# Expert rows moved by DMA through DRAM instead of by one-hot products, in a two-block transformer kernel

## Chip, cores and metric

One core of a Trainium2 chip runs the kernel. The metric is the device time in microseconds of one execution; three runs of the kernel before gave 2006.03, 2007.79 and 2010.1 us, so the median is 2007.79 us.

## What is computed

The reference runs 256 tokens of width 1024 through two transformer layers of one model and one layer of a second, all in float32. The part that the change touches is the feed-forward of the second layer, a mixture of experts: each token goes to two of eight experts, the tokens of an expert are collected in blocks of 128 rows, each block is multiplied by its expert's weights, and the results are weighted and added back to their tokens.

```python
logits = (xt @ w_router).astype(jnp.float32)
top_logit, top_idx = lax.top_k(logits, TOP_K)
gates = jax.nn.softmax(top_logit, axis=-1)
...
dest = pad_start[sorted_e] + (jnp.arange(A, dtype=jnp.int32) - start[sorted_e])
tok_buf = jnp.full((rows,), T, jnp.int32).at[dest].set((order // TOP_K).astype(jnp.int32))
gate_buf = jnp.zeros((rows,), jnp.float32).at[dest].set(gates.reshape(-1)[order])
...
xs = xt_pad[tok_buf].reshape(n_blocks, EXPERT_BLOCK, D)

def expert_block(args):
    xb, e = args
    return swiglu(xb, w_gate[e], w_up[e], w_down[e])

ys = lax.map(expert_block, (xs, block_expert)).reshape(rows, D)
ys = ys * gate_buf[:, None].astype(ys.dtype)
out = jnp.zeros((T + 1, D), ys.dtype).at[tok_buf].add(ys)[:T]
```

The expert width is 3584, so an expert has 42 units of weights of 1 MB. The inputs shown here need eight blocks, one for each expert; up to eleven are provided for.

## The kernel before, in words

**Precision.** Every large product is made from three products of a shorter type: SyncE loads a unit of weights (128x2048) into one of six slots of `raw`, ScalarE writes its high part `wh` (L922 in the expert loop, L638 elsewhere), VectorE subtracts to get the low part `wl` (`rest`, L1495), and TensorE multiplies high by high, low by high and high by low (L1047 to L1049). The high and low parts have three slots. SyncE may refill a slot when the split of its unit is done (`lo_ready`); ScalarE may split unit j+3 when TensorE is done with unit j (`unit_done`); TensorE waits for `lo_ready` of each unit.

**Order of work.** All engines have their instructions written out in order. Attention and feed-forward (L1223 to L1228, called FFN0 here) of the first layer come first; between FFN0's units SyncE also loads 24 units `ada` for VectorE's modulation vectors (L1691), which use the same ring. FFN0's list of loads runs g0 u0 g1 u1 d0 ada0 ada1 ada2 g2 u2 d1 ada3 ada4 g3 u3 d2. Then come the second layer's convolution and attention, its router, and the expert loop, followed by the second model.

**Before the loop.** `z_tok` (tokens in rows) comes from transposes (`ztok`). VectorE works out for each token's two assignments a row number `kcol`, 128 times the block plus the row in it. TensorE turns `kcol` and the gates `gcol` into rows (`as_rows`, L1300, for `krow` and `grow`).

**One-hot products.** `select` (L1842 to L1854) compares `kcol` with 0 to 127, giving a matrix `sel` with a one where a token belongs to a row of this block, then takes 128 off `kcol` for the next block. `gather` (L1306 to L1311) multiplies `z_tok` by `sel`, 16 products of 128x128 in two halves (banks `G0`, `G1`), and leaves the block's rows transposed in PSUM; ScalarE and VectorE split them into `xgh` and `xgl`. For the way back, VectorE builds `scat` (L1925 to L1932), a matrix of gates at the places of the tokens, and `scatter` (L1324 to L1328) multiplies the block's result `y_tok` by it: eight products of 128x256 in four groups (`S0` to `S3`). VectorE adds each group to the residual `hT` (L1907).

**The loop** (TensorE L1332 to L1401, ScalarE L916 to L945, VectorE L1889 to L1938, SyncE L531 to L535) runs over the blocks. A block has seven chunks c; each has two units of gate (g), two of up (u) and, one chunk later, two of down (d) weights: g0 u0 g1 u1 d0 g2 u2 d1 and so on to d6, each in two halves. After the first gate units of the next chunk TensorE transposes the hidden state (`turned`, L1354, banks `T0` to `T6`), ScalarE takes its high and VectorE its low part. The scatter groups of the block before stand behind the up units of chunks 0 to 3 (L1391 to L1395); both gather halves for the next block stand behind `d5` (L1396 to L1401), the second of them in the PSUM bank that the last transpose `T6` used, so that it waits until VectorE has drained it. At the end of a block ScalarE copies the result from PSUM into `y_tok` (L944). After the loop TensorE scatters the last block (L1403 to L1409), and POOL, ScalarE and VectorE go on with the second model.

POOL does nothing in the loop: it clears `y_tok` and `scat` at L599 and L600, and its next instruction (L603) waits for the last scatter.

## Time and profile before

| | before |
|---|---|
| runs | 2006.03, 2007.79, 2010.1 us |
| median | 2007.79 us |
| span of the profiled execution | 2008.4 us |
| TensorE busy | 1882.3 us, 94% |
| VectorE busy | 1484.6 us, 74% |
| ScalarE busy | 1173.2 us, 58% |
| POOL busy | 177.5 us, 9% |
| DMA of SyncE's queue | 497.24 MB, 65.7% of 16 engines' span |
| chain that ended last | TensorE 83%, VectorE 7%, ScalarE 5% |
| mean granted TensorE clock | 0.971 of full |

For the profiled execution no time of its own is given beside its span; the span is 0.6 us above the median of the runs. Busy times count overlapping matmuls once. "Idle before" is the time an engine stood still ahead of an instruction, with the instruction whose end released it. A float32 matmul shows as two records, one of the shorter type or a transpose as one. Times of instructions are microseconds from the start of the span.

### The profile page before, as it was taken

Reading aid. Unit: us, or ns where it says so; the run is one execution under the profiler, and the core shown is the slowest. Engines: PE = TensorE matmul, PEld = TensorE weight load, DVE = VectorE, ACT = ScalarE, POOL = GpSimd, SP = SyncE. Lnnn points to the kernel's source line nnn. Section 1 sums busy time; section 2 is a strip of 40 time slices with the busy share of each in tenths; the row PEclk is TensorE's granted clock in tenths of the full one; section 3 lists DMA queues with packets and bytes.
Section 4 is the critical chain, followed back from the end, with each engine's and each line's share of the span. In section 5 each row is a group of like instructions: output and inputs, shape, how many; then the busy total and the mean of one; then the engine's idle time right before and its main releaser. Section 6 shows DMA issues by size and latency. Waiting matters only on the chain.

```text
span 2008.4 us, 28246 instructions
## 1 busy us (share of the span) xinstructions
PE 1882.3 (94%) x10934; PEld 1656.0 (82%) x10934; DVE 1484.6 (74%) x1406; ACT 1173.2 (58%) x1143; POOL 177.5 (9%) x156
## 2 busy tenths in 40 slices
PE   6988999999789999999999999999999979679997
PEld 6977999998778788788787887878878879569997
DVE  6856777667668979798797897887979845665554
ACT  5445434448446767767676777767777744643332
POOL 3032111211000000000000000000000000312221
PEclk8999999999879999999999999999999979999999
DMA  7404788730239979899798998997989934024540
GB/s 296 135 14 158 280 328 335 273 126 1 105 126 354 368 297 355 313 357 364 305 347 327 351 361 310 359 371 293 357 310 361 367 130 167 23 105 161 178 166 22
DMA packets 69052, 499.89 MB, mean 249 GB/s; under 512 B 7664, under 2 KB 7792, under 8 KB 8432
## 3 DMA queue, kind: packets, MB, share of 16 engines
q1 hardware_dynamic: 68688, 497.24, 65.7%
q0 software_dynamic: 288, 1.57, 0.2%
q8 instruction: 55, 0.90, 0.2%
q14 instruction: 21, 0.17, 0.0%
HBM read 497.73 MB, written 1.05 MB: 248 GB/s over the span
## 4 chain that ended last, share of the span: by engine, by line
PE 83%; DVE 7%; ACT 5%; issue 3%; POOL 1%; DMA 0%; DVEq 0%; ACTq 0%; SPq 0%
PE ps L1047 24%; PE ps L1049 24%; PE ps L1048 24%; ACT wh L922 2%; DVE wl L1495 2%; PE ps L1327 2%; PE ps L1249 2%; PE ps L1070 2%; PE ps L1309 1%; DVE big L1488 1%; PE ps L1354 1%; POOL xl L556 1%; PE ps L1178 1%; DVE al L1495 1%; PE ps L1199 1%
## 5 line engine op out<-in xcount | busy, mean ns | idle before, releaser
L1495 DVE TENSOR_TENSOR wl<-raw,wh 128x2048 fp32r<-128x2048 f32 x446 | 1021.4, 2292 | 321.2 <-ACT wh L638 177.2
L922 ACT ACTIVATE wh<-raw 128x2048 fp32r<-128x2048 f32 x336 | 643.0, 1918 | 229.8 <-PE ps L1049 229.8
L1047 PE MATMUL ps<-wh,xh 128*128 128x512 f32 (+1 forms) x1040 | 398.1, 383 | 2.6 <-DVE wl L1495 2.6
L1049 PE MATMUL ps<-wh,xl 128*128 128x512 f32 (+1 forms) x1040 | 390.7, 376 | 0.0
L1048 PE MATMUL ps<-wl,xh 128*128 128x512 f32 (+1 forms) x1040 | 389.7, 375 | 0.0
L1047 PE MATMUL ps<-xh,wh 128*128 128x256 f32 x1184 | 346.1, 292 | 30.4 <-POOL xl L556 14.5
L1048 PE MATMUL ps<-xl,wh 128*128 128x256 f32 x1184 | 341.4, 288 | 0.0
L1049 PE MATMUL ps<-xh,wl 128*128 128x256 f32 x1184 | 341.2, 288 | 0.0
L638 ACT ACTIVATE wh<-raw 128x2048 fp32r<-128x2048 f32 x107 | 204.2, 1910 | 175.0 <-PE ps L1049 171.1
L1047 PEld LDWEIGHTS ps<-xh,wh 128*128 128x128 f32 x1184 | 233.0, 197 | 35.8 <-issue 30.0
L1048 PEld LDWEIGHTS ps<-xl,wh 128*128 128x128 f32 x1184 | 233.1, 197 | 1.7 <-issue 1.7
L1049 PEld LDWEIGHTS ps<-xh,wl 128*128 128x128 f32 x1184 | 232.6, 196 | 0.0
L1047 PEld LDWEIGHTS ps<-wh,xh 128*128 128x128 f32 x1040 | 195.9, 188 | 41.2 <-DVE wl L1495 7.2
L1049 PEld LDWEIGHTS ps<-wh,xl 128*128 128x128 f32 x1040 | 195.8, 188 | 36.1
L1048 PEld LDWEIGHTS ps<-wl,xh 128*128 128x128 f32 x1040 | 196.0, 189 | 34.4 <-issue 1.0
L1047 PE MATMUL ps<-wh,ah 128*128 128x512 f32 x448 | 181.7, 406 | 1.6 <-DVE al L1495 1.6
L1049 PE MATMUL ps<-wh,al 128*128 128x512 f32 x448 | 175.4, 391 | 0.0
L1048 PE MATMUL ps<-wl,ah 128*128 128x512 f32 x448 | 175.0, 391 | 0.0
L1047 PE MATMUL ps<-ah,wh 128*128 128x256 f32 x432 | 122.4, 283 | 0.2 <-POOL al L587 0.2
L1048 PE MATMUL ps<-al,wh 128*128 128x256 f32 x432 | 122.3, 283 | 0.0
L1049 PE MATMUL ps<-ah,wl 128*128 128x256 f32 x432 | 122.3, 283 | 0.0
L550 POOL MEMSET big<- 128x4096 f32 (+1 forms) x3 | 8.0, 2665 | 1082.4 <-DVE hT L1670 1082.1
(276 smaller groups left out, 2161.1 us busy)
## 6 DMA issues: line engine op xcount, KB each, us to landing
raw<-in_experts SPq DMA_DIRECT2D x336, 1024.0 KB, 4.8
raw<-in_units SPq DMA_DIRECT2D x134, 1024.0 KB, 5.1
big<-in_mem SPq DMA_DIRECT2D x1, 1024.0 KB, 7.1
hT<-in_x SPq DMA_DIRECT2D x1, 1024.0 KB, 9.1
big<-in_mem POOLq DMA_DIRECT2D x1, 1024.0 KB, 7.1
out<-sqz SPq DMA_DIRECT2D x2, 512.0 KB, 2.6
cst<-in_constants SPq DMA_DIRECT2D x1, 752.5 KB, 14.4
big<-in_c POOLq DMA_DIRECT2D x1, 512.0 KB, 7.9
```

The source lines that it names most:

```text
L556: pool.tensor_tensor(xl[:, k, :], src[:, k, :], xh[:, k, :].bitcast(F32), ALU.subtract).then_inc(sem("norm_lo_pool"), 1)
L638: act.activation(wh[:, p % SPL, :], raw[:, n % RAW, :], ACT.Copy).then_inc(sem("hi_ready"), 1)
L922: act.activation(wh[:, p % SPL, :], raw[:, n % RAW, :], ACT.Copy).then_inc(sem("hi_ready"), 1)
L1047: mm(out_, lh, rh, start=start, stop=False, **kw)
L1048: mm(out_, lh, rl, start=False, stop=False, **kw)
L1049: return mm(out_, ll, rh, start=False, stop=stop, **kw)
L1070: ins = mm(bank(f"nsum{k}")[:, 0:T], ones, src[:, T * j:T * j + T], start=(j == 0), stop=(j == KT - 1))
L1178: ins = mm(s[:, at:at + nk], m["q"][:, P * t:P * t + P], m["k"][:, 0:nk], start=True, stop=not fox)
L1199: mm(o[:, 0:T], m["v"][0], pT[:, 0:T], start=not second, stop=False, skip_group_check=True)
L1249: mm(bank(f"conv{c}")[:, 0:T], diag[:, n % DIAG_RING, :], upad[:, c, tap:tap + T], start=(tap == 0), stop=(tap == TAPS - 1)).then_inc(sem( ...
L1327: ins = mm(psum[:, T * c:T * c + T], y_tok[:, P * o:P * o + P], scat, start=True, stop=True)
L1495: return V.tensor_tensor(out_, whole, leading.bitcast(F32), ALU.subtract)
```

## The change

Rows go through two new tensors in DRAM, `x_rows` and `y_rows`, of twelve blocks of 128 rows each. Only the first block is still gathered with a one-hot product, and only the last is still scattered with one.

- SyncE fills all twelve blocks of `x_rows` and five of `y_rows` with zeros, in two DMAs from a cleared stretch of SBUF, behind the load of `u2` in FFN0. POOL's clearing of the convolution's padding now covers 1716 columns in place of 180.
- Before the loop POOL scatters the token rows to `x_rows` in four indirect DMAs (two assignments by two halves of the tokens).
- In each block SyncE stores the result of the block before (behind its thirteenth load) and loads the rows of the next block into `x_blk` (behind its twenty-first). TensorE turns these with eight transposes where the gather stood. The scatter groups, the token adds and the per-block `select` and `scat` work are gone from the loop; `scat` is made once before it, for the last block.
- During the last block POOL gathers every assignment's result row from `y_rows` (four indirect DMAs), scales by the gates, with zero for rows of the last block, and adds both; TensorE adds these tokens transposed into the banks of the last scatter.
- `as_rows("krow")` now stands behind the first gather; `select` no longer waits for it. The last scatter's groups use the banks 6, 7, 4, 5.

The core of the diff:

```diff
@@ SyncE
                 load(n)
+                if n == NUMBER["u2"]:
+                    sp.wait_ge(sem("upad_zeroed"), 1)
+                    sp.dma_start(x_rows.rearrange("a p f -> p a f"),
+                                 zeros.unsqueeze(1).broadcast_to([P, MAXBLK + 1, D])).then_inc(sem("rows_zeroed"), 16)
+                    sp.dma_start(y_rows[E - 1:MAXBLK + 1, :, :].rearrange("a p f -> p a f"),
+                                 zeros.unsqueeze(1).broadcast_to([P, MAXBLK + 2 - E, D])).then_inc(sem("rows_zeroed"), 16)
...
                 load_expert(j, slice(0, 1))
+                if j == 20:
+                    sp.wait_ge(sem("x_scattered"), 16 * 2 * TT)
+                    sp.dma_start(x_blk, x_rows[1:2, :, :].rearrange("a p f -> p (a f)"))
...
                     load_expert(j, bass.ds(e, 1))
+                    if j == 12:
+                        sp.wait_ge(sem("moe_y"), i * 2 + 3)
+                        sp.dma_start(y_rows[bass.ds(i, 1), :, :].rearrange("a p f -> p (a f)"), y_tok)
+                    if j == 20:
+                        sp.wait_ge(sem(f"moe_filled{b}"), i * per + use + 1)
+                        sp.dma_start(x_blk, x_rows[bass.ds(i + 2, 1), :, :].rearrange("a p f -> p (a f)"))
@@ POOL
-            pool.memset(y_tok, 0.0).then_inc(sem("moe_y"), 1)
-            pool.memset(scat, 0.0).then_inc(sem("moe_scat"), 1)
+            pool.wait_ge(sem("rows_zeroed"), 32)
+            pool.wait_ge(sem("moe_rows"), 1)
+            for a in range(2):
+                for t in range(TT):
+                    pool.indirect_dma_start(x_by_row, IndirectOffsetOnAxis(kidx[:, a, t:t + 1], 0), z_tok[:, t, :], None)
...
+            pool.wait_ge(sem("y_stored"), last * 16 + 1)
...
+            for t in range(TT):
+                for a in range(2):
+                    pool.indirect_dma_start(y_got[a][:, t, :], None, y_by_row, IndirectOffsetOnAxis(yidx[:, a, t:t + 1], 0))
+            for t in range(TT):
+                pool.wait_ge(sem(f"y_got{t}"), 32)
+                pool.tensor_scalar(y_got[0][:, t, :], y_got[0][:, t, :], gkept[:, 0, t:t + 1], None, ALU.mult)
+                pool.tensor_scalar(y_got[1][:, t, :], y_got[1][:, t, :], gkept[:, 1, t:t + 1], None, ALU.mult)
+                pool.wait_ge(sem("y_gated"), 2 * t + 2)
+                pool.tensor_tensor(y_kept[:, t, :], y_got[0][:, t, :], y_got[1][:, t, :], ALU.add)
@@ ScalarE
+                act.wait_ge(sem("y_stored"), i * 16 + 1)
                 for g in range(2):
                     act.activation(y_tok[:, 512 * g:512 * g + 512], ps[:, 4 + g, :], ACT.Copy)
@@ TensorE
+            def tokens_of_earlier_blocks(psum, j):
+                for c in range(2):
+                    o = 2 * j + c
+                    for t in range(TT):
+                        at = T * c + P * t
+                        mm(psum[:, at:at + P], y_kept[:, t, P * o:P * o + P], ident, start=(c == 0 and t == 0), stop=False,
+                           skip_group_check=True)
...
+                def next_rows(g):
+                    psum, done = spare(f"G{g}")
+                    for f in range(4):
+                        at = 512 * g + P * f
+                        ins = pe.transpose(psum[:, P * f:P * f + P], x_blk[:, at:at + P], ident)
+                    ins.then_inc(done, 1)
...
-                    if (kind, half) == ("u", 1) and c < 4:
-                        if c == 0:
-                            pe.wait_ge(sem("moe_y"), i * 2 + 1)
-                            pe.wait_ge(sem("moe_scat"), i + 1)
-                        scattered(c)
                     if (kind, c, half) == ("d", MOE_CH - 2, 1):
                         turned(MOE_CH - 1)
-                        pe.wait_ge(sem("moe_sel"), i * TT + 2 * TT)
+                        pe.wait_ge(sem("x_loaded"), i * 16 + 16)
                         for g in range(2):
-                            psum, done = spare(f"G{g}")
-                            gather(psum, g).then_inc(done, 1)
+                            next_rows(g)
...
+            pe.wait_ge(sem("y_kept"), TT)
             for j in range(4):
+                if j == 2:
+                    pe.wait_ge(sem("moe_y"), nb * 2 + 1)
                 claim(pe, f"scat{j}")
+                tokens_of_earlier_blocks(bank(f"scat{j}"), j)
+            pe.wait_ge(sem("moe_scat"), 1)
+            for j in range(4):
                 scatter(bank(f"scat{j}"), j).then_inc(filled(f"scat{j}"), 1)
@@ VectorE
             dve.wait_ge(sem("upad_zeroed"), 1)
+            dve.wait_ge(sem("rows_zeroed"), 32)
...
-            wait_filled(dve, "krow")
-            select(0, first=True)
...
+            V.tensor_copy(kidx[:, :, :], kcol[:, :, :]).then_inc(sem("moe_rows"), 1)
...
+            link(V.tensor_scalar(pexp[:, 9:10], pexp[:, 8:9], -1.0, float(CAP), ALU.add, ALU.mult))
+            link(V.tensor_scalar(kept[:, :, :], kcol[:, :, :], pexp[:, 9:10], None, ALU.is_lt))
+            V.tensor_tensor(gkept[:, :, :], gcol[:, :, :], kept[:, :, :], ALU.mult).then_inc(sem("moe_kept"), 1)
+            link(V.tensor_tensor(kfl[:, :, :], kcol[:, :, :], kept[:, :, :], ALU.mult))
+            V.tensor_copy(yidx[:, :, :], kfl[:, :, :]).then_inc(sem("moe_kept"), 1)
...
+            link(V.tensor_scalar(krow[:, 0:2, :], krow[:, 0:2, :], pexp[:, 9:10], None, ALU.subtract))
+            link(stt(scat, krow[:, 0, :], sid, krow[:, 2, :], ALU.is_equal, ALU.mult))
+            link(stt(scat_b, krow[:, 1, :], sid, krow[:, 3, :], ALU.is_equal, ALU.mult))
+            V.tensor_tensor(scat, scat, scat_b, ALU.add).then_inc(sem("moe_scat"), 1)
...
-                    if (kind, half) == ("u", 1) and c < 4:
-                        add_tokens(c)
-                    if (kind, c, half) == ("g", 3, 0):
-
-                        select(i + 1)
-                    if (kind, c, half) == ("g", 4, 0):
-
-                        stt(scat, krow[:, 0, :], sid, krow[:, 2, :], ALU.is_equal, ALU.mult).then_inc(sem("scat_half"), 1)
-                        stt(scat_b, krow[:, 1, :], sid, krow[:, 3, :], ALU.is_equal,
-                            ALU.mult).then_inc(sem("scat_half"), 1)
...
```

## Rows read from the trace of the kernel before

**Rows 1.** TensorE in the expert loop by line: xcount, busy and mean, idle before.
```profile
L1047 PE MATMUL ps<-wh,xh 128*128 128x512 f32 x896 | 355.5, 397 | 2.6 <-DVE wl L1495 2.6
...
L1047 PE MATMUL ps<-wh,ah 128*128 128x512 f32 x448 | 181.7, 406 | 1.6 <-DVE al L1495 1.6
...
L1309 PE MATMUL ps<-big 128*128 128x128 f32 x256 | 38.3, 312 | 21.6 <-DVE al L1495 21.6
```

**Rows 2.** TensorE in order of time: start, length, line, operation; around two scatters.
```profile
723.66 1.02 PE L1327 MATMUL ps<-big 128*128 128x256 f32 x4
724.52 0.50 PE L1047 MATMUL ps<-wh,xh 128*128 128x512 f32 x1
...
736.04 1.02 PE L1327 MATMUL ps<-big 128*128 128x256 f32 x4
...
737.36 0.40 PE L1049 MATMUL ps<-wh,al 128*128 128x512 f32 x1
```

**Rows 3.** VectorE in order of time: feed-forward stage, and start of block 2.
```profile
230.47 3.00 DVE L1495 TENSOR_TENSOR wl<-raw,wh 128x2048 fp32r<-128x2048 f32 x1 [0.30 <-ACT wh L638]
...
722.18 4.49 DVE L1495 TENSOR_TENSOR wl<-raw,wh 128x2048 fp32r<-128x2048 f32 x2 [1.42 <-ACT wh L922]
```

**Rows 4.** TensorE in order of time, ends of block 1 and block 2.
```profile
698.02 0.60 PE L1354 MATMUL ps<-cst,att_p 128*128 128x128 f32 x4
698.46 1.95 PE L1309 MATMUL ps<-big 128*128 128x128 f32 x16
703.12 3.68 PE L1309 MATMUL ps<-big 128*128 128x128 f32 x16 [2.70 <-DVE al L1495]
...
833.94 2.05 PE L1309 MATMUL ps<-big 128*128 128x128 f32 x16 [2.71 <-DVE al L1495]
835.75 0.48 PE L1047 MATMUL ps<-wh,ah 128*128 128x512 f32 x1
```

**Rows 5.** Stretches: length, busy PE, PEld, DVE, ACT, POOL, PEclk, DMA share, GB/s.
```profile
703.00:706.50 3.50, 3.38 (x16) 3.39 (x17) 0.66 (x2) 0.00 (x0) 0.00 (x0) 0.52 1.00 403
833.90:837.30 3.40, 3.36 (x23) 3.11 (x24) 1.22 (x2) 0.60 (x1) 0.00 (x0) 1.00 0.95 395
...
740.00:757.70 17.70, 17.70 (x82) 14.63 (x81) 15.33 (x10) 12.45 (x9) 0.00 (x0) 1.00 0.94 359
```

**Rows 6.** TensorE in order of time, from the key rows to the first unit.
```profile
571.49 2.07 PE L1300 MATMUL ps<-cst,kcol 128*128 128x128 f32 x8 [2.71 <-DVE kcol L1836]
575.06 6.30 PE L1309 MATMUL ps<-big 128*128 128x128 f32 x32 [1.49 <-DVE big L1488]
```

**Rows 7.** The page's DMA issues: KB each, us to landing.
```profile
raw<-in_experts SPq DMA_DIRECT2D x336, 1024.0 KB, 4.8
raw<-in_units SPq DMA_DIRECT2D x134, 1024.0 KB, 5.1
...
out<-sqz SPq DMA_DIRECT2D x2, 512.0 KB, 2.6
```

**Rows 8.** SyncE, ScalarE and TensorE in order of time, first feed-forward stage.
```profile
208.72 0.33 SPq L507 DMA_DIRECT2D raw<-in_units  x1
...
228.53 1.90 ACT L638 ACTIVATE wh<-raw 128x2048 fp32r<-128x2048 f32 x1
...
238.32 0.28 PE L1047 MATMUL ps<-ah,wh 128*128 128x256 f32 x1
...
244.09 0.28 PE L1047 MATMUL ps<-xh,wh 128*128 128x256 f32 x1
```

**Rows 9.** POOL in order of time.
```profile
228.71 2.61 POOL L587 TENSOR_TENSOR al<-att_p,ah 128x512 fp32r<-128x512 f32 x1 [13.53 <-ACT ah L799]
...
1720.06 0.92 POOL L572 TENSOR_SCALAR att_p<-att_p,rsum 128x256 f32<-128x256 f32 x1
```

**Rows 10.** TensorE in order of time, from the last unit to the scatters.
```profile
1625.53 6.68 PE L1327 MATMUL ps<-big 128*128 128x256 f32 x16 [3.35 <-ACT big L944]
```

**Rows 11.** VectorE's waits in total: us, times, longest.
```profile
DVE wl L1495 <- ACT wh L922: 140.7, 193, 4.6
```

More of the change, by code:

```diff
@@ L228, in build @@
         plan_f = sb("plan_f", [P, 16, 16])
+        kidx = sb("kidx", [P, 2, TT], U32)
+        yidx = sb("yidx", [P, 2, TT], U32)
+        kept = sb("kept", [P, 2, TT])
+        gkept = sb("gkept", [P, 2, TT])
+        kfl = sb("kfl", [P, 2, TT])
+        marks = sb("marks", [P, 4])
         lt8 = sb("lt8", [P, E, E])
@@ L265, in build @@
         y_tok = big[:, 2048:3072]
+        x_blk = big[:, 3072:4096]
+        zeros = big[:, 0:D]
+        upad_flat = big[:, 0:CT * (PAD + T)]
+        y_got = [view(0, TT, D), view(5888, TT, D)]
+        y_kept = y_got[0]
         krow = view(4096, 4, T)
@@ L393, in build @@
         for j in range(4):
-            S.add(f"scat{j}", 4 + j)
+            S.add(f"scat{j}", (6, 7, 4, 5)[j])
         S.add("nsum5", 0)
@@ L580, in _ @@
             zero_keys(mkz1, "keys1_zeroed")
[L581 removed]
+            pool.memset(upad_flat, 0.0).then_inc(sem("upad_zeroed"), 1)
             subtract_hi("ffn0")
@@ L1318, in _ @@
                 gather(bank(f"gather{j}"), j).then_inc(filled(f"gather{j}"), 1)
+            as_rows("krow", kcol)
             pe.wait_ge(sem("moe_plan"), 2)
@@ L1326, in scatter @@
                     o = 2 * j + c
-                    ins = mm(psum[:, T * c:T * c + T], y_tok[:, P * o:P * o + P], scat, start=True, stop=True)
+                    ins = mm(psum[:, T * c:T * c + T], y_tok[:, P * o:P * o + P], scat, start=False, stop=True,
+                             skip_group_check=True)
                 return ins
```

75 lines of the change are left out of this document (41 added, 34 removed).

## Prediction

> **What bounds the kernel now.** I read the page first (engine shares, then the chain that ended last), then the groups of the expert loop on TensorE, then that engine in order of time around each piece the change touches, and last the queues. The loop over eight expert blocks runs from 582 to 1622 us, so 130.0 us a block, and TensorE is idle in it for hardly more than its waits: 21.6 us in eight waits before the second gather product, 2.6 and 1.6 us elsewhere [rows 1]. TensorE is the bound of this stretch; what leaves TensorE's order leaves the time, unless the next weights are not split yet. In the stretch between two scatter products VectorE is busy 15.33 of 17.70 us and the DMA engines 0.94 [rows 5]: both follow closely.
>
> **Scatter products leave the loop.** From the start of one (736.04) to the third matmul behind it (737.36) are 1.32 us; two ordinary steps of 0.23 us are in that, so a scatter costs 0.87 us [rows 2]. At the head of blocks 2 to 8 it hides something, though: the first scatter runs 723.66 to 724.52, and the split of the weights that TensorE wants next comes from a pair of VectorE subtractions, 722.18 for 4.49 us, the first of which ends near 724.4 [rows 2, 3]. Without the scatter TensorE waits there instead: 0.1 us saved. Sum: 24 x 0.87 + 0.87 (block 1 starts with its splits ahead) + 7 x 0.1 = 22.5 us. The bounds are 0.1 and 0.87 each; I take the upper one for the later three, since blocks' later chunks, which have no scatter, run without a wait for a split (2.6 us in seven waits, all at block starts [rows 1]). The waits of 0.2 us for the hidden state's low part (1.6 us in eight [rows 1]) come where VectorE builds the scatter matrix; that work goes before the loop: 1.5 us saved. The selection, the token adds and the key steps on VectorE were beside TensorE: nothing by themselves.
>
> **Gather products become eight transposes.** The order is transpose (698.02), first gather (698.46), a wait of 2.70 us, second gather (703.12), next unit. In a block at full clock the second gather holds the next unit for 1.81 us (833.94 to 835.75) [rows 4]. Four transposes take 0.44 us (698.02 to 698.46), so 1.37 us go. The first gather saves nothing: the wait ends when VectorE has drained the last hidden state, which does not hang on the gather, so the wait grows from 2.7 to about 4.2 us. That has a price: in four of the eight such stretches, one of each kind shown, the granted clock fell to its lower level of 1.2 GHz (a mean of 0.52 against 1.00 [rows 5]) and the gather took about 3.4 us (3.68 with its tail [rows 4]). After the change the half clock would fall on 0.44 us of transposes and then on the unit's matmuls, costing some 1.7 us (half of 3.4). Before: 4 x 1.81 + 4 x 3.4 = 20.8 us. After, with a longer wait, I take half clock in seven of eight: 8 x 0.44 + 7 x 1.7 = 15.4. Saved 5 us; 17 if the clock never falls, 3.7 if always.
>
> **Before the loop.** Selecting no longer waits for the key rows, so the first gather starts some 2.4 us earlier, but the key rows now stand behind it, and VectorE copies them before it splits the gathered rows. The stretch from 571.49 [rows 6] to the loop's first unit at 582 keeps all its products and loses a wait of 1.5 us; the copy and one split (0.7 us each) then stand before the first unit. -0.5 us, between -2 and +1. The new small VectorE steps (about 0.2 us each) and four for the scatter matrix (some 2 us) lie beside TensorE's gathers and first units. Four scattering DMAs on POOL and four row transfers run beside block 1; SyncE waits for them only behind its twenty-first load, an estimated 14 units of 2.8 us past 582, near 621 us.
>
> **The zero fill in the first feed-forward stage.** 17 pieces of 512 KB are 8.9 MB. The output's 512 KB stores land as writes in 2.6 us each [rows 7]; the bulk rate in the loop is 395 GB/s at a share of 0.95 [rows 5], near 404 at a full share, so 22 us in SyncE's own queue, ahead of every later weight load. The load before it is issued at 208.72 and lands 5.1 us later [rows 7, 8]; the next load would land at 213.8 + 22 + 2.6 = 238.4. ScalarE takes it at 228.53 today, TensorE at 238.32 [rows 8]. With 1.90 us for the high part and 2.25 for the low part it is ready at 242.6: 4.3 us late. Three loads on, at 246.2, the unit TensorE wants at 244.09 + 4.3 is ready at 250.4: 2.0 more. Together 6 us; the bounds are 0 and the whole 22, and I take the worked-out value. SyncE's wait for the cleared columns costs nothing: POOL clears them long before, when it has no other work.
>
> **Transfers in the loop.** One store and one load of 512 KB a block add 1.05 MB to 44.0. A load is issued when a slot's split ends, 12.5 us before ScalarE needs it (six units of 2.8 less the 4.2 of a split), and lands after 4.8 us [rows 7]: nearly 8 us of cover against 1.3 us each. Free; if the cover is gone, 2.6 us a block. The 45.1 MB in a block of 126.3 us need 357 GB/s, and rows show 395 [rows 5]. The Trainium skill, page "DMA: Bandwidth & Descriptors", section Specifications, puts HBM for one core at about 358 GB/s. By that rate a block could not go under 126.0 us, so it would leave this sum as it is but cut off every result below mine; the trace disagrees, its rows being above that rate already.
>
> **POOL in the last block.** When the rows of the first seven blocks are in DRAM, POOL fetches them (four indirect DMAs) and runs four scalings and two additions of 128x1024 while the last block multiplies. POOL has a hundred microseconds for that, so its own length is free. What is not free is VectorE: beside POOL's subtraction (228.71) a split took 3.00 us, where two in a row take 4.49, and POOL, which had started under another split, lasted to 231.32 [rows 3, 9]. The two took turns: the 128x512 subtraction needed about 1.15 us after VectorE's ended. So an addition of 128x1024 holds VectorE for 2.3 us. A scaling of 128x256 takes 0.92 [rows 9]; by columns 3.7 us for 1024, at the subtraction's rate 2.3, and I take 2.8. Sum 4 x 2.8 + 2 x 2.3 = 15.8 us. Alternating with six splits this spans 30 us, in which VectorE has 13% free (2.37 us of 17.70 [rows 5]), so 3.8 us, and a split has about 1 us of lead. TensorE loses 11 us; bounds 0 and 16.
>
> **The tail.** TensorE stood idle for 3.35 us for the last rows' copy, then ran the scatters for 6.68 us at half clock [rows 10]. The earlier blocks' tokens add 16 products of 128 columns: eight fit into that idle time, eight stand behind it, 1.8 us at full and 3.4 at half clock. If the fuller order keeps the clock up, the scatters shrink to 3.4. +1 us, between -1.5 and +3.5.
>
> **Sum.** -22.5 - 1.5 - 5 - 0.5 + 6 + 11 + 1 = -11.5 us. The profiled execution's span is 2008.4 us, 0.6 above the runs' median of 2007.8; so 1996.9 for the span and 1996 as the median, 0.6% faster. A difference of 0.2%, 4 us, is what a measurement of this kernel can tell from none.
>
> **Rivals.** *POOL fits into VectorE's gaps*: without the 11 us, 1985. For it: VectorE waits 140.7 us for ScalarE's high parts over the loop [rows 11]. Against: the 3.00 us split. Chance 0.20. *The zero fill is fully exposed*, its writes slower or the stage's loads never catching up: 22 in place of 6, 2012. Against: the ring of six loads. 0.10. *The clock stays up*: gather saves 17, 1984. 0.07. *Slower: the splits become the bound everywhere in the loop*, as at the head of a block: then no scatter saves more than 0.1 us, 22.5 becomes 3, and the time is 2016. It decides once a split ends less than 0.9 us ahead of the unit that follows a scatter; against it, the scatterless chunks. 0.05. *Slower: an indirect DMA of 128 rows is dear.* SyncE's queue stands behind the first four; from about 573 to 630 us they may take 14 us each before loads come late, and beyond 17 us each the gain of 11.5 is gone. The nearest row, POOL's direct 512 KB, issues in under 1 us. 0.05. My forecast holds 0.53 within 1988 to 2004. That rows do not move as described I hold to be excluded, since the old products are deleted.
>
> **Chances.** Faster by over 0.2%: the forecast nearly all, POOL in gaps, clock up: 0.78. Within 0.2%: its upper edge and the zero fill: 0.12. Slower: both slow rivals: 0.10. The range 1982 to 2012 leaves out the slower two and little else.
>
> **What would show it.** Scatter lines only at the end; chunks of 16.8 us in place of 17.7; a wait of about 4.2 us before the second group of row transposes in each block, half clock behind most; two waits of TensorE for weights between 235 and 255 us; in the last block VectorE's splits at over 4 us beside POOL and TensorE waiting some 11 us; the tail longer by 1. I am wrong if blocks 2 to 7 do not shorten by about 3.3 us, or if ScalarE waits for loads in the loop.

## Result, and the profile after

The changed kernel takes 1983.37 us (median of four runs, 1982.42 to 1988.2), the kernel before 2006.91 in the same comparison (2004.31 to 2010.1). The ratio is 0.9882, with a 95% interval from 0.987 to 0.9893: 23.5 us or 1.2% faster. The forecast of 1996, 11.5 us faster, has the right sign and half the size; 1983.4 lies just inside its range and outside the 1988 to 2004 that its main case named. The profiled execution's span is 1981.4 us against 2008.4 before.

TensorE in the expert loop by line, the view that gave [rows 1], and below it that engine's waits from 585 to 1600 us (in total, times, longest):

```profile
L1111 PE MATMUL ps<-wh,xh 128*128 128x512 f32 x896 | 355.6, 397 | 9.4 <-DVE wl L1570 8.9 <-DVE xl L1570 0.6
...
L1111 PE MATMUL ps<-wh,ah 128*128 128x512 f32 x448 | 181.5, 405 | 0.8 <-DVE wl L1570 0.8
L1112 PE MATMUL ps<-wl,ah 128*128 128x512 f32 x448 | 179.9, 402 | 0.0
...
L1427 PE MATMUL ps<-cst,att_p 128*128 128x128 f32 x224 | 33.6, 272 | 0.0
```

```profile
PE ps L1435 <- DVE al L1570: 32.4, 8, 4.1
PE ps L1111 <- DVE wl L1570: 9.6, 16, 1.4
```

In the kernel before, the third of these groups was:

```profile
L1048 PE MATMUL ps<-wl,ah 128*128 128x512 f32 x448 | 175.0, 391 | 0.0
```

The gather and scatter products are gone from the loop. The groups of the gate and up units are what they were (355.6 against 355.5 us in the first). Two of the three groups of the down units, which follow a block's last transposes, take 4.9 and 4.1 us more (175.0 to 179.9 here, 175.4 to 179.5 for high by low): the half clock that fell on gather products before now falls on them. The eight waits before the second part of the gather are now eight waits before the second four transposes, and have grown from 21.6 to 32.4 us. The waits for weights have grown from 2.6 in seven to 9.6 in sixteen. The waits of 1.6 us for `al` before the down units are gone.

The end of block 1, in order of time, and the granted clock around it (columns as in [rows 5]):

```profile
697.08 0.60 PE L1427 MATMUL ps<-cst,att_p 128*128 128x128 f32 x4
697.51 0.60 PE L1435 MATMUL ps<-cst,big 128*128 128x128 f32 x4
702.17 1.12 PE L1435 MATMUL ps<-cst,big 128*128 128x128 f32 x4 [4.06 <-DVE al L1570]
```

```profile
700.80:707.60 6.80, 5.43 (x16) 4.44 (x17) 2.61 (x4) 0.60 (x1) 0.00 (x0) 0.52 0.73 295
```

In and behind the wait of 4.06 us the clock stands at its lower level, and it falls so at all eight block ends (four of eight before): for 6.8 us at the ends of blocks 1, 4 and 8, for 3.4 us at the others. Block 4 takes 126.8 us, 0.7 more than its neighbours. Two whole blocks, the seventh and the eighth, in which GpSimd works:

```profile
1343.80:1470.00 126.20, 121.07 (x541) 99.22 (x540) 104.69 (x58) 91.86 (x64) 0.00 (x0) 0.99 0.92 357
1470.00:1600.00 130.00, 122.71 (x548) 99.59 (x546) 110.17 (x58) 91.77 (x63) 31.30 (x11) 0.97 0.93 363
```

A block is taken from one copy of the outputs into `y_tok` to the next. Blocks 2 to 7 take 126.0 to 126.8 us (before: 129.1 to 130.7), the last 130.1 (before: 132.1).

The DMA issues, as in [rows 7]:

```profile
raw<-in_experts SPq DMA_DIRECT2D x336, 1024.0 KB, 6.7
...
x_rows<-big SPq DMA_DIRECT2D x1, 6144.0 KB, 21.0
big<-x_rows SPq DMA_DIRECT2D x8, 512.0 KB, 7.8
y_rows<-big SPq DMA_DIRECT2D x7, 512.0 KB, 6.7
y_rows<-big SPq DMA_DIRECT2D x1, 2560.0 KB, 25.7
...
x_rows<-big,kidx POOLq DMA_INDIRECT x4, 3.7
big<-y_rows,yidx POOLq DMA_INDIRECT x4, 11.5
```

A load of expert weights lands 1.9 us later than before (6.7 against 4.8), and no engine waits for it in the loop.

**Where the time went.** ScalarE takes its 446 splits in the same order in both kernels, so the start of the same split in the two traces tells where they part. All times in us:

| stretch | before | after | gain or loss | forecast |
|---|---|---|---|---|
| start to FFN0 | to 191.29 | to 191.84 | +0.55 | 0 |
| FFN0, with the zero fill | to 371.50 | to 377.61 | +5.56 | +6 |
| from there to the second attention | to 494.98 | to 499.00 | -2.09 | 0 |
| router, preparation, first units of the loop | to 588.76 | to 591.78 | -1.00 | -0.5 |
| the eight blocks to the last output copy, GpSimd's six operations left out (first experiment) | 1035.27 | 1004.51 | -30.76 | -29 |
| GpSimd's six operations | | 1008.28 | +3.77 | +11 |
| from the last output copy to the last split | 353.07 | 350.02 | -3.05 | +1 |
| sum | 1977.10 | 1950.08 | -27.02 | -11.5 |

The medians differ by 23.5 us; the other 3.5 lie in the choice of the profiled executions. A run's time is about 2 us above its span, so the span of 2008.4 belongs to the slowest of the four runs before, 2010.1. Of the 15.5 us between the two last columns GpSimd makes 7.2 (too dear), the tail 4.1, a stretch that the change doesn't touch (371 to 495 us) 2.1, and the loop 1.8.

The untouched stretch holds the same TensorE instructions in every kernel here (785), and its length goes with the granted clock. It is 121.47 us at a mean clock of 0.99 in experiment 6. The kernel before and experiment 4 (columns as in [rows 5]):

```profile
371.50:494.98 123.48, 119.05 (x785) 109.05 (x784) 82.37 (x129) 75.20 (x158) 25.93 (x22) 0.97 0.33 118
```

```profile
378.64:499.17 120.53, 116.08 (x785) 106.49 (x784) 82.41 (x129) 74.53 (x159) 25.97 (x22) 1.00 0.33 122
```

The same holds of the second model, behind the last scatter: its instructions are the same in the thirteen traces, and they take 343.4 to 346.2 us. Of the tail's 3.05 us, 1.50 lie there (345.06 to 343.56), and 1.56 between the last output copy and the second model's first product (8.02 to 6.46).

### The profile page after: what moved, and what is told of

Same layout as the page of the kernel before. It is cut to its first block, busy times and chain, and to the rows that moved or that the text cites. A ratio compares the mean times of both kernels' runs of the same rounds, so it can differ in the third digit from the quotient of the medians.

```text
span 1981.4 us, 27648 instructions
## 1 busy us (share of the span) xinstructions
PE 1837.5 (93%) x10646; PEld 1613.3 (81%) x10646; DVE 1453.4 (73%) x1311; ACT 1173.0 (59%) x1143; POOL 213.1 (11%) x171
## 4 chain that ended last, share of the span: by engine, by line
PE 82%; DVE 7%; ACT 6%; issue 3%; DMA 2%; POOL 1%; ACTq 0%; DVEq 0%; SPq 0%
PE ps L1111 24%; PE ps L1113 24%; PE ps L1112 24%; DVE wl L1570 2%; ACT wh L985 2%; PE ps L1313 2%; PE ps L1134 2%; DMA raw<-in_units 1%; PE ps L1427 1%; DVE big L1563 1%; POOL xl L589 1%; PE ps L1242 1%; PE ps L1263 1%; ACT L996 0%; ACT L985 0%
## 5 line engine op out<-in xcount | busy, mean ns | idle before, releaser
L1112 PE MATMUL ps<-wl,ah 128*128 128x512 f32 x448 | 179.9, 402 | 0.0
L1113 PE MATMUL ps<-wh,al 128*128 128x512 f32 x448 | 179.5, 401 | 0.0
L620 POOL TENSOR_TENSOR al<-att_p,ah 128x512 fp32r<-128x512 f32 x27 | 74.9, 2773 | 325.9 <-ACT ah L862 325.9
```

The lines of the kernel that those rows point to most:

```text
L620: pool.tensor_tensor(al[:, c % 2, :], sg[:, c % 2, :], ah[:, c % 2, :].bitcast(F32), ALU.subtract).then_inc(sem("hid_lo"), 1)
L1112: mm(out_, lh, rl, start=False, stop=False, **kw)
L1113: return mm(out_, ll, rh, start=False, stop=stop, **kw)
```

## Experiments

Eleven kernels, each with the kernel before on the same chip; ratios are to that. The changed kernel was not run again beside them. The kernel before had medians of 2008.17 (experiments 1, 3, 4, 5), 2009.26 (2, 6, 9, 10) and 2008.26 (7, 8, 11), against 2006.91 in the first comparison, so a difference of medians to the changed kernel is good to some 2 us; smaller ones are read from stretches of the traces.

### 1. GpSimd's six operations left out

```diff
             for t in range(TT):
                 pool.wait_ge(sem(f"y_got{t}"), 32)
-                pool.tensor_scalar(y_got[0][:, t, :], ..., gkept[:, 0, t:t + 1], None, ALU.mult)
-                pool.tensor_scalar(y_got[1][:, t, :], ..., gkept[:, 1, t:t + 1], None, ALU.mult)
-                pool.wait_ge(sem("y_gated"), 2 * t + 2)
-                pool.tensor_tensor(y_kept[:, t, :], y_got[0][:, t, :], y_got[1][:, t, :], ALU.add)
...
-            pe.wait_ge(sem("y_kept"), TT)
+            for t in range(TT):
+                pe.wait_ge(sem(f"y_got{t}"), 32)
```

> The changed kernel without GpSimd's six operations in the last block: the gates and the second expert's rows are left out of the tokens of blocks 1 to 7. The theory after the result (the scalings give way to VectorE and only the two additions hold it): TensorE loses only the 1.38 and 0.76 us that it waited for splits at 1517 and 1530 us, so 2 to 4 us less, 1979.5 to 1981.5. The forecast's term (VectorE held for 15.8 us, TensorE loses 11): 11 us less, about 1972.

Measured: 1981.87 us (1980.33 to 1982.85), ratio 0.9864 [0.9846, 0.9882], 1.5 us less than the changed kernel. By the trace the last block falls from 130.1 to 126.2 us, the length of its neighbours; this execution reached the loop 2.6 us later than the changed kernel's (594.39 against 591.78), with nothing changed before it. VectorE's splits in the last block, changed kernel and experiment:

```profile
L1570 DVE TENSOR_TENSOR wl<-raw,wh 128x2048 fp32r<-128x2048 f32 x42 | 101.6, 2428 | 18.7 <-ACT wh L985 18.5
```

```profile
L1564 DVE TENSOR_TENSOR wl<-raw,wh 128x2048 fp32r<-128x2048 f32 x44 | 100.7, 2290 | 26.1 <-ACT wh L978 26.1
```

GpSimd lengthens 42 splits by 138 ns each on average, 5.8 us in all. TensorE's waits in the changed kernel's last block that its neighbours don't have:

```profile
1518.44 0.50 PE L1111 MATMUL ps<-wh,xh 128*128 128x512 f32 x1 [1.38 <-DVE wl L1570]
...
1531.22 0.50 PE L1111 MATMUL ps<-wh,ah 128*128 128x512 f32 x1 [0.76 <-DVE wl L1570]
```

They are 2.1 us. By the starts of its 42 splits, the block falls 3.2 us behind the one before it between the 17th and the 23rd, where GpSimd works, and the other 0.7 of its 3.9 us at its end, where the clock stands at its lower level for 6.8 us in place of 3.4. Block 4, in which GpSimd does nothing, has the same 0.7, so it isn't shown to be GpSimd's. In experiments 3 and 4 GpSimd does all six operations, the clock at the last block's end is as at the other ends, and that block is longer by 3.2 us alone. The forecast had 15.8 us of hold and 11 us lost. That value is ruled out; the theory's 2 to 4 holds by the trace (3.8), and the median lies 0.4 us above its range.

### 2. Scalings left out, additions kept

```diff
-                pool.tensor_scalar(y_got[0][:, t, :], ..., gkept[:, 0, t:t + 1], None, ALU.mult)
-                pool.tensor_scalar(y_got[1][:, t, :], ..., gkept[:, 1, t:t + 1], None, ALU.mult)
-                pool.wait_ge(sem("y_gated"), 2 * t + 2)
                 pool.tensor_tensor(y_kept[:, t, :], y_got[0][:, t, :], y_got[1][:, t, :], ALU.add)
```

> The changed kernel without GpSimd's four scalings by the gates (the gates are left out), the two additions kept. The last block takes 130.1 us in the changed kernel's trace and 126.2 without all six operations, and VectorE's splits beside the six are 5.8 us longer. Theory (the additions hold VectorE, the scalings mostly wait for it): the block stays at 129 or more, 1982.5 to 1983.5. Rival (the scalings hold it as much): 127.5 or less, 1981.

Measured: 1981.66 us (1981.02 to 1984.02), ratio 0.9861 [0.9844, 0.9877]. The medians can't part the two cases here (1.7 us less than the changed kernel); the trace can. The last block:

```profile
1470.40:1600.20 129.80, 122.66 (x548) 99.88 (x547) 108.22 (x58) 91.80 (x63) 14.79 (x7) 0.97 0.92 364
```

```profile
1507.18 3.26 POOL L657 TENSOR_TENSOR big<-big 128x1024 f32<-128x1024 f32 x1 [4.12 <-DMA big<-y_rows,yidx]
1514.69 2.97 POOL L657 TENSOR_TENSOR big<-big 128x1024 f32<-128x1024 f32 x1 [4.25 <-DMA big<-y_rows,yidx]
```

130.1 us with all six operations, 129.8 with two additions alone, 126.2 with nothing: the four scalings cost 0.3, the two additions up to 3.6. By the starts of the splits, which leave out the clock at the block's end, it is 0.5 and 2.7.

### 3. Zero fill in the attention stage

```diff
-        zeros = big[:, 0:D]
+        zeros = al[:, :, :].rearrange("p a b -> p (a b)").bitcast(F32)
...
-                if n == NUMBER["u2"]:
-                    sp.wait_ge(sem("upad_zeroed"), 1)
+                if n == NUMBER["u0"]:
+                    sp.wait_ge(sem("al_zeroed"), 1)
...
             subtract_hi("x")
+            pool.memset(zeros, 0.0).then_inc(sem("al_zeroed"), 1)
...
             subtract_hi("ffn0")
+            pool.wait_ge(sem("rows_zeroed"), 32)
```

> The changed kernel with the zero fill issued at about 100 us, in the attention stage, where no load runs. Theory: the fill costs 5.5 us in the first feed-forward network and nothing here, 1983.4 - 5.5 = about 1978, and TensorE's two waits for weights between 235 and 255 us are gone. Rival (the 3 us won between 260 us and the loop are the fill's own delay paid back): only 2.5 less, about 1981. Second rival (the fill delays attention, or GpSimd's clearing does): no gain.

Measured: 1978.68 us (1976.77 to 1979.59), ratio 0.9848 [0.983, 0.9867], 4.7 us less than the changed kernel. SyncE issues the fill right behind the last load before attention:

```profile
96.94 0.33 SPq L522 DMA_DIRECT2D raw<-in_units  x1
97.31 0.43 SPq L539 DMA_DIRECT2D x_rows<-al  x1
97.78 0.66 SPq L541 DMA_DIRECT2D y_rows<-al  x1
```

TensorE's waits from 180 to 300 us in the changed kernel, and in the experiment:

```profile
PE ps L1111 <- DVE wl L1570: 5.0, 1, 5.0
PE ps L1111 <- POOL xl L589: 4.3, 1, 4.3
```

```profile
PE ps L1113 <- POOL xl L589: 4.3, 1, 4.3
```

The wait for weights is gone; the other was there all along. The stretch of FFN0, 185.8 us in the changed kernel, takes 180.2 as before. The second rival falls. The first had a sign in this trace: from FFN0 to the second attention it takes 123.5 us where the changed kernel takes 121.4. But the same stretch takes 121.4 in experiment 10, which has the early fill, and 121.5 in experiments 6 to 8, which have none, so it does not hang on the fill, and the first rival falls too.

### 4. The last transposition one unit earlier

On all three engines the last chunk's `turned`, `turned_hi` and `turned_lo` move from behind d5's second unit to behind its first:

```diff
-                    if (kind, c, half) == ("d", MOE_CH - 2, 1):
+                    if (kind, c, half) == ("d", MOE_CH - 2, 0):
                         turned(MOE_CH - 1)
+                    if (kind, c, half) == ("d", MOE_CH - 2, 1):
                         pe.wait_ge(sem("x_loaded"), i * 16 + 16)
                         for g in range(2):
                             next_rows(g)
```

> The changed kernel with the last chunk's transposition (TensorE, ScalarE and VectorE) one unit earlier, behind d5.0 instead of d5.1. Theory: the 4.1 us in which TensorE waits for the al split before the second four transposes of each block are slack of the order of work, and the half clock that follows costs 1 to 1.7 us more; both go in all eight blocks: 8 x (4.1 + 0.5 to 1) = 37 to 41 us less, 1942 to 1947. Rival: the splits or the loads, which catch up in that wait, become what TensorE waits for at the next block's head, and 10 us or less are won, 1973 or more.

Measured: 1950.43 us (1949.0 to 1951.17), ratio 0.9709 [0.9691, 0.9727], 32.9 us less than the changed kernel. Blocks 2 to 7 take 121.8 us, all six within 0.03. TensorE's waits from 585 to 1563 us, and block 2:

```profile
PE ps L1436 <- DVE al L1572: 10.3, 8, 1.3
PE ps L1112 <- DVE wl L1572: 9.7, 16, 1.4
```

```profile
707.90:829.80 121.90, 119.52 (x542) 98.04 (x542) 104.59 (x58) 91.86 (x64) 0.00 (x0) 1.00 0.95 370
```

The wait fell from 4.1 to 1.3 us, not to nothing, and the clock no longer falls at the end of any block. Of 4.4 us a block, 2.8 are wait and the other 1.6 clock. The waits for weights stayed at 9.7, so the splits do not take over (rival), though each block now draws 370 GB/s. By the traces the eight blocks take 971.7 us in place of 1008.3, 36.6 less; the second model, in which nothing was edited, takes 2.7 more, at a lower mean clock. The theory of 37 to 41 was too high, since it let the wait go entirely.

### 5. The kernel before without the scatter products

The products and VectorE's additions in the loop are deleted, and their places in the order of the banks' uses with them; `select`, `scat` and the gather stay.

```diff
-                    if (kind, half) == ("u", 1) and c < 4:
-                        if c == 0:
-                            pe.wait_ge(sem("moe_y"), i * 2 + 1)
-                            pe.wait_ge(sem("moe_scat"), i + 1)
-                        scattered(c)
...
-                    if (kind, half) == ("u", 1) and c < 4:
-                        add_tokens(c)
```

> The kernel before without the scatter products and the additions to the tokens in the loop (the tokens of all blocks but the last are left out), the gather by products kept. The forecast's term: 22.5 us less than before, about 1984.5. Rival (the scatter is worth less, since splits that hid behind the products now show, and the gather's change brought the rest): 16 or less, 1991 or more. Second rival (VectorE's additions, too, were on the path): 27 or more, 1980 or less.

Measured: 1988.5 us (1987.21 to 1989.64), ratio 0.9897 [0.9879, 0.9915]. The eight blocks take 1014.9 us instead of 1035.3 by the traces: 20.4. TensorE's waits in the loop:

```profile
PE ps L1309 <- DVE al L1490: 21.6, 8, 2.7
PE ps L1047 <- DVE wl L1490: 7.5, 14, 0.7
PE ps L1047 <- DVE al L1490: 1.6, 8, 0.2
```

The waits for weights rose from 2.6 in seven to 7.5 in fourteen: seven new waits of 0.7, which the scatter at the head of blocks 2 to 8 had hidden, as the forecast had it. Blocks at full clock take 126.5 (129.2 before), blocks in which the clock falls 128.0 (130.6 before): 2.7 or 2.6 us for the four scatters of a block, against 3 x 0.87 + 0.1 = 2.7 in the forecast. The median (19.7 less) lies between forecast and first rival. The sum fell 2 us short, since the clock fell in six blocks here and in four before.

### 6. The kernel before with transposes for the gather

```diff
                             psum, done = spare(f"G{g}")
-                            gather(psum, g).then_inc(done, 1)
+                            for f in range(4):
+                                at = 512 * g + P * f
+                                ins = pe.transpose(psum[:, P * f:P * f + P], z_tok[:, 0, at:at + P], ident)
+                            ins.then_inc(done, 1)
```

> The kernel before with the gather's 32 products in each block replaced by eight transposes of the first rows of the tokens (the selection is left out, so that later blocks get the wrong tokens), the scatter kept. The forecast's term: 5 us less than before, plus 1.5 for the al split, about 2001. Theory after the run without scatter products (the seven blocks lost 25.0 us in the changed kernel, 16.3 with the scatter alone gone, so the gather is worth 8.7 in seven): 9 to 11 us less, about 1998. Rival (the rest of the gain came from VectorE's operations in the loop, the selection and the scatter matrix): 3 or less, 2005.

Measured: 2001.5 us (1999.16 to 2003.42, six runs), ratio 0.9962 [0.9949, 0.9974]: 7.8 us less. By the traces 2.0 us lie ahead of the first changed instruction and 2.3 behind the loop; the eight blocks take 4.5 us less, though the clock now falls at the end of all eight. The forecast's 5 holds, and the theory that I had formed from the previous run (9 to 11, by subtraction) falls: subtracting one part from the whole gave the gather what belongs to both together.

### 7. The kernel before with neither

Experiments 5 and 6 in one kernel, with none of the change's transfers.

```diff
...
-                        scattered(c)
...
-                        add_tokens(c)
...
-                            gather(psum, g).then_inc(done, 1)
...
+                                ins = pe.transpose(psum[:, P * f:P * f + P], z_tok[:, 0, at:at + P], ident)
```

> The kernel before without the scatter products and with the gather's products replaced by eight transposes (earlier blocks' tokens and the selection are left out), and with none of the change's transfers. Alone, the scatter was worth 20.4 us of the eight blocks in the traces and the gather 4.6; the changed kernel won 30.7 without GpSimd's operations. Theory (the two do not add up: without the scatter most gathers ran at half clock, where their products cost 1.6 us more a block, and transposes cost hardly any): blocks of 126.2 us as in the changed kernel, 30 us less than before, about 1978, which also says that the transfers in the loop cost nothing. Rival 1 (they add up and the changed kernel won the other 6 us elsewhere): blocks of 126.9 or more, 1983 or more. Rival 2 (the transfers in the loop cost the changed kernel time): blocks of 125.5 or less, 1972 or less.

Measured: 1977.96 us (1976.94 to 1981.37), ratio 0.985 [0.9832, 0.9868]. Blocks 2 to 8 take 126.3 to 126.7 us and one of them 127.9; all eight take 28.2 us less than before, where the parts alone give 20.4 + 4.5 = 24.9. The waits:

```profile
PE ps L1398 <- DVE al L1493: 32.4, 8, 4.1
PE ps L1047 <- DVE wl L1493: 7.4, 14, 0.7
PE ps L1047 <- DVE al L1493: 1.6, 8, 0.2
```

The same 32.4 us as in the changed kernel. The last line is the 1.6 us that the changed kernel doesn't have, because VectorE no longer builds `scat` in the loop; with it the 28.2 are 29.8, against 30.8 there. So the transfers in the loop cost nothing that shows (rival 2 falls), and the parts do not add up (rival 1 falls). With transposes the clock falls at every block's end. They are worth 1.3 to 1.6 us in a block in which it fell with gather products too (130.6 to 129.3 with the scatters, 128.0 to 126.4 without) and nothing in one in which it had not (129.2 to 129.3, 126.5 to 126.4). With the scatters gone and the gather kept it falls in six blocks instead of four, for a reason that no run settles.

### 8. The kernel before with the last transposition earlier

The edit of experiment 4 on the kernel before, in `turned`, `turned_hi` and `turned_lo`:

```diff
-                    if (kind, c, half) == ("d", MOE_CH - 2, 1):
+                    if (kind, c, half) == ("d", MOE_CH - 2, 0):
                         turned(MOE_CH - 1)
+                    if (kind, c, half) == ("d", MOE_CH - 2, 1):
                         pe.wait_ge(sem("moe_sel"), i * TT + 2 * TT)
```

> The kernel before with the last chunk's transposition one unit earlier, everything else kept. Theory: its wait of 2.7 us for the al split before the second part of the gather goes and the clock stays up, blocks of 126.3 instead of 129.2 to 130.7, 8 x 3.4 = 27 us less, about 1981; the change is then worth 4.5 us a block (126.3 - 121.8) instead of 3.7, since the gather's products fill less of a wait. Rival (the splits are further behind in this kernel and TensorE waits for weights instead): 10 us less or fewer, 1998 or more.

Measured: 1977.88 us (1977.02 to 1978.4), ratio 0.9846 [0.983, 0.9863]. Every block takes 126.4 us, the clock falls in none, and no wait for `al` is left before the gather. From 850 to 980 us:

```profile
850.00:980.00 130.00, 129.43 (x598) 106.72 (x597) 112.63 (x73) 95.09 (x66) 0.00 (x0) 1.00 0.92 349
```

This one move of a transposition brings the kernel before 30 us, more than the whole change does. With it, a block of the changed kernel (121.8) is 4.6 us shorter than one of the kernel before (126.4); without it blocks 2 to 7 differ by 3.4 on average.

### 9. The tail with its wait left empty

```diff
+            pe.wait_ge(sem("moe_y"), nb * 2 + 1)
             for j in range(4):
-                if j == 2:
-                    pe.wait_ge(sem("moe_y"), nb * 2 + 1)
                 claim(pe, f"scat{j}")
```

> The changed kernel with all 32 token products of the tail behind the wait for the last block's outputs, so that TensorE idles for 3 us there as it did before. Theory (the changed kernel gains in its tail because the products that fill the wait keep the clock up): token and scatter products run at half clock, 5 to 7 us more, 1988 to 1990. Rival (the clock has nothing to do with it, only the 2 us of products filling the wait count): 2 us more, 1985.5.

Measured: 1986.95 us (1985.41 to 1988.12), ratio 0.9887 [0.987, 0.9903]: 3.6 us more than the changed kernel by the medians, and 3.4 by the traces from the last output copy to the second model's first product (9.88 against 6.46). TensorE in the tail, changed kernel and experiment:

```profile
1598.04 1.95 PE L1393 MATMUL ps<-cst,big 128*128 128x128 f32 x16
1601.17 2.05 PE L1393 MATMUL ps<-cst,big 128*128 128x128 f32 x16 [1.19 <-ACT big L1008]
1603.06 3.62 PE L1399 MATMUL ps<-big 128*128 128x256 f32 x16
```

```profile
1601.81 5.46 PE L1393 MATMUL ps<-cst,big 128*128 128x128 f32 x32 [2.97 <-ACT big L1008]
1607.11 3.62 PE L1399 MATMUL ps<-big 128*128 128x256 f32 x16
```

The kernel before idled 3.35 us and ran the same sixteen products in 6.68 us at half clock [rows 10]. In the changed kernel half of the token products fill the wait, it is 1.19 us long, the clock stays up and the scatters take 3.62. With the wait left empty the clock falls, but the half clock lands on part of the token products (5.46 in place of 4.0 us) and has passed before the scatters. So both readings had a part: 1.8 us are the longer wait, 1.5 the clock. The 5 to 7 of the theory were too much. The kernel before, too, need not pay in full: in experiments 6 to 8 the same sixteen scatter products behind the same wait took 5.38 us, since the clock was up again before their end.

### 10. Zero fill and transposition together

```diff
-                if n == NUMBER["u2"]:
+                if n == NUMBER["u0"]:
...
-                    if (kind, c, half) == ("d", MOE_CH - 2, 1):
+                    if (kind, c, half) == ("d", MOE_CH - 2, 0):
                         turned(MOE_CH - 1)
```

> The changed kernel with both edits, the zero fill in the attention stage and the last chunk's transposition one unit earlier. Theory (they touch different stages): 33.0 and 4.7 us add up, 1983.4 - 37.7 = about 1945.7. Rival (part of the fill's gain is taken back by the loop or was scatter between runs): 1948 or more.

Measured: 1940.37 us (1939.32 to 1942.19), ratio 0.9659 [0.9643, 0.9676]: 69 us less than before and 43 less than the changed kernel, 5 more than the sum of the two. By the traces the excess is 6 us: 2.0 in FFN0, 1.2 between it and the second attention, 3.0 in the tail, none in the loop. In the last two nothing was edited; they are stretches whose length goes with the granted clock, and most of the 3.0 is the 2.7 by which the second model was long in experiment 4. Why the clock fell less often here no run shows. It keeps the whole computation and is the fastest version found.

### 11. The additions given to TensorE

On the version of experiment 10, TensorE adds the two scaled rows itself:

```diff
-                pool.wait_ge(sem("y_gated"), 2 * t + 2)
-                pool.tensor_tensor(y_kept[:, t, :], y_got[0][:, t, :], y_got[1][:, t, :], ALU.add)
...
-                        mm(psum[:, at:at + P], y_kept[:, t, P * o:P * o + P], ident, ...)
+                        for a in range(2):
+                            mm(psum[:, at:at + P], y_got[a][:, t, P * o:P * o + P], ident, ...)
```

> The version with the early zero fill and the early last transposition (1940.4 us), and GpSimd's two additions given to TensorE, which adds both scaled rows with 16 more products against the identity in each half of the tail. Theory: VectorE is free of the additions, the last block falls from 125.0 to 122.1, 2.9 us less; the tail pays 32 products of 0.128 us, of which 1.2 us fill its wait, 2.9 more: no change, 1939.5 to 1941.5. Rival (the scalings, now without the additions between them, hold VectorE as well): 2 to 3 us more, 1943.

Measured: 1940.88 us (1938.5 to 1944.45), ratio 0.9664 [0.9644, 0.9684]: no change, as the theory had it. The last block and the one before it, and in the last one a scaling with the splits beside it:

```profile
1433.20:1555.10 121.90, 119.58 (x550) 98.31 (x550) 105.64 (x58) 91.90 (x63) 26.43 (x9) 1.00 0.97 389
1311.36:1433.24 121.88, 119.56 (x541) 98.02 (x540) 104.58 (x58) 91.87 (x63) 0.00 (x0) 1.00 0.96 369
```

```profile
1477.04 5.05 POOL L659 TENSOR_SCALAR big<-big,gkept 128x1024 f32<-128x1024 f32 x1 [0.19 <-DMA big<-y_rows,yidx]
```

```profile
1477.17 5.32 DVE L1572 TENSOR_TENSOR wl<-raw,wh 128x2048 fp32r<-128x2048 f32 x2
```

Two splits run beside this scaling in 5.32 us, where two in a row take 4.49 [rows 3]. Four scalings cost VectorE 1.1 us in all (105.64 against 104.58 busy) and TensorE nothing: the block is as long as its neighbour to 0.02 us. The 3.2 us that the additions cost there go. The 16 products more make the way from the last output copy to the second model 2.1 us longer (8.58 against 6.46); the 1.0 us left is less than the runs differ by.

## Why the prediction was half right

**Scatter products (-22.5): right.** Alone 20.4 us; 2.6 to 2.7 in a block of like clock. The waits of 0.7 us that appeared at each block's head are what the 0.1 us for the first scatter of a block stood for.

**Waits for `al` (-1.5): right**, 1.6 us.

**Gather (-5): right**, 4.5 alone. The wait grew to 4.1 us (4.2 forecast) and the clock fell at eight block ends of eight (seven), on transposes and units as forecast. Together with the two above, the loop won 30.8 us where 29 were forecast.

**Zero fill (+6): right in size, partly by luck.** 5.6 by the trace, 4.7 by the medians of experiment 3. The load behind it reached ScalarE at 238.34 (238.4 forecast). TensorE waited 5.02 us once, where the forecast had 4.3 and then 2.0: the second wait never came. In the rest the stretch's clock has a part, which stood lower for 3.4 us more than before.

**Loop transfers (0): right.** Blocks with and without them (experiment 7) differ by 0.2 us, the other way at that, which is the wait for `al` that the one without them keeps. The rule cited from the Trainium skill, page "DMA: Bandwidth & Descriptors", section Specifications, some 358 GB/s for a core, is no bound here: a block of 121.9 us draws 370 GB/s, and the last one of experiment 11 389.

**GpSimd in the last block (+11): the step that failed.** The price per operation was wrong for one of its two kinds. "An addition of 128x1024 holds VectorE for 2.3 us" came from a two-input operation and was near: the splits beside the two took 2.2 and 1.6 us longer. "By columns 3.7 us for 1024 ... and I take 2.8" gave a scaling of one input the same hold, from its own duration, though no row showed a scaling beside a split. Four of them hold VectorE for 1.1 us in experiment 11 and 2.0 in the changed kernel (the 5.8 less 2.2 and 1.6 beside the additions); it is they that stretch. In the changed kernel:

```profile
1510.44 3.12 POOL L659 TENSOR_SCALAR big<-big,gkept 128x1024 f32<-128x1024 f32 x1
1513.65 2.58 POOL L662 TENSOR_TENSOR big<-big 128x1024 f32<-128x1024 f32 x1
1516.23 7.00 POOL L657 TENSOR_SCALAR big<-big,gkept 128x1024 f32<-128x1024 f32 x1
```

The same scaling takes 3.1 to 7.0 us, by what VectorE does beside it. The two splits that the additions held:

```profile
1513.90 4.49 DVE L1570 TENSOR_TENSOR wl<-raw,wh 128x2048 fp32r<-128x2048 f32 x1
1527.28 3.89 DVE L1570 TENSOR_TENSOR wl<-raw,wh 128x2048 fp32r<-128x2048 f32 x1
```

The second step was off the other way: 5.8 us of hold less 3.8 for VectorE's free time and 1 for the lead would leave TensorE 1 us, and it lost 3.2, since the additions' holds of 2.2 and 1.6 us come at once and not spread over 30 us. (The block's other 0.7 us are the clock at its end, as in block 4.) With the hold right and this step as it stood the forecast would have been too low. The rival in which POOL fits into VectorE's gaps, 1985, had the better number, though not by its mechanism: the splits did take 5.8 us longer.

The Trainium skill, page "SBUF — State Buffer", section "SBUF: two separate sides", has an exclusive lock on a shared port between a VectorE operation with two inputs in SBUF and a GpSimd operation that reads SBUF, held for the whole instruction by whichever starts first. For the additions the traces agree: the splits that started 2.33 and 1.74 us before the additions of 2.58 us ended took 2.20 and 1.60 us longer. As a price for scalings it doesn't serve: by their shortest record, 3.12 us, four would hold VectorE for 12 us, and they held it for 1.1 to 2.0.

**Tail (+1): wrong by 2.6.** From the last output copy to the second model's first product the changed kernel takes 6.46 us and the kernel before 8.02, so -1.6. The scatters shrink by 3.1 (6.68 to 3.62), the token products behind the wait add 1.9, and the wait ends 0.4 sooner. The step was "if the fuller order keeps the clock up, the scatters shrink to 3.4": it stood in the text as an end of the range (-1.5) and should have been the value taken, since the waits behind which [rows 4, 5] show half clock are of 2.70 us, in four of eight, and the filled wait is 1.19. The other 1.5 us of the table's -3.05 lie in the second model, where nothing changed.

**Before the loop (-0.5): -1.0**, and 2.1 more between 371 and 495 us, where nothing changed. Experiments 6, 7 and 8, whose instructions up to there are those of the kernel before, show the same 2.0, experiment 5 none. It is a difference between executions, by the clock, not the change's. With the 1.5 in the second model, 3.6 us of the traces' 27.0 come from such differences.

## What to carry to other kernels

A wait that a moved or shortened operation uncovers is worth more attention than the operation: here taking products out of the loop won 30.8 us of it, and moving one transposition a unit earlier won as much again. Where one engine's instructions lengthen those of another, as GpSimd's did VectorE's, price each kind of instruction by a row in which that kind runs beside the other engine's, not by its own duration. Parts of a change measured alone need not add up where TensorE's clock answers to the idle between them.

## What the runs showed of the hardware that was not expected

- GpSimd's scaling of 128x1024 (one input tensor, a scalar per partition) beside VectorE's two-input subtraction takes 3.1 to 7.0 us and costs VectorE 0.3 to 0.5 on average; its addition (two inputs) takes 2.6 to 3.3 and costs it 1.6 to 2.2: the split beside the first addition took 4.49 us in place of 2.29, the one beside the second 3.89.
- Four indirect DMAs of 128 rows of 4 KB each kept GpSimd for 0.99, 2.01, 2.27 and 2.42 us when they fetched rows and for about 1 us each when they wrote them, and landed after 11.5 and 3.7 us beside the weight loads.
- With GpSimd's transfers added, the DMA engines moved 421 GB/s from 1510 to 1527 us at a full share, and weights still came in time.
- Programs that are the same up to 580 us reached 584 to 595 us up to 3.0 us apart (583.85 and 586.85 in experiments 10 and 3), by where the granted clock fell on the way: one stretch of the same instructions took 120.5, 121.5 and 123.5 us at a mean clock of 1.00, 0.99 and 0.97. A difference of 2 us between two single traces says nothing unless the stretch is one that the change touches.
